# Input norm from row sums of 32 columns and a first conditioning chunk loaded ahead of the activations, in a one-core transformer layer

## The chip, the core and the metric

The kernel runs on one core of a Trainium2 chip. The metric is the device time of one execution in microseconds, from the start of the program to its end. All data is f32, and an f32 matmul appears in the trace as two passes (two MATMUL records with two weight loads).

## What is computed

One layer of a diffusion backbone over 256 latent tokens and 256 context tokens of width 1024: a modulated RMS norm, three token mixing branches (neighbourhood attention, a gated scan, grouped-query attention) from one projection, a gated merge, and then a mixture of 16 experts with the top 2 per token. The change touches only the very first step:

```python
mod   = split((silu(c)     @ w_ada + b_ada), 6)      # c: conditioning of the sample
mod_c = split((silu(c_ctx) @ w_ada + b_ada), 6)      # c_ctx: that of the context
h_lat = modulate(rmsnorm(x,   g_mix), mod[0],   mod[1])
h_ctx = modulate(rmsnorm(ctx, g_mix), mod_c[0], mod_c[1])
# rmsnorm(x, g) = x * rsqrt(mean(x*x) + 1e-6) * g ;  modulate(h, shift, scale) = h * (1 + scale) + shift
y_lat = token_mixer(h_lat, h_ctx, w_in, ...)
```

## The kernel before, in words

Everything is written out by hand: five instruction streams (SyncE issues the large transfers, GpSimd, ScalarE, TensorE, VectorE), held together by semaphores. Each stream runs strictly in its written order, so a wait holds back all that is written behind it on that engine.

The activations of both token sets lie transposed in `hT`: 128 partitions, 8 slices k of the width, 512 tokens (256 latent, 256 context). The front works like this:

- Transfers (L418 to L425, SyncE): four chunks of `xcT` (two slices k each, 512 KB), and then, four times, a conditioning chunk `ada_mix[g]` (2048 KB, the weights that give shift and scale for the slices 2g and 2g+1) with a quarter of the first projection's weights, "ff" (512 KB). The conditioning vectors `cvec` and the first part of the small tables come over ScalarE's queue (L598, L599).
- Squares: ScalarE squares the even slices (L602), VectorE the odd ones (L1285), into `sq`.
- Sums: TensorE sums over the 128 partitions by a matmul with a 128 x 128 block of ones (L998), 8 slices into `pv_bank`. Every partition of the result holds the sum of all 512 tokens.
- Root and reciprocal: ScalarE takes `sqrt(sum/1024 + eps)` over 512 columns (L609), VectorE the reciprocal of 512 columns (L1287). Before, ScalarE has turned `cvec` into its Silu (L604) and has loaded the table of Sqrt with an operation on one column (L606).
- Conditioning: `mix(g)` (L977) is 8 matmuls with 32 columns of weights, in four column groups of the array side by side, over 512 moving columns; ScalarE copies the result out of the bank (L614), `mix_turn(g)` (L986) turns it by four transposes, and VectorE makes from it the shift `mod` and the factor `A_mix` (L1310 to L1316).
- Norm and modulation (VectorE): each slice times the reciprocal row (L1308), then times factor plus shift for the two halves of the tokens (L1321), which raises `h_ready`.
- The first projection, "ff" (L1019): for each k four matmuls i of 512 columns; `mix(g+1)` is put behind the first of them in a group of two slices, `mix_turn(g+1)` ahead of the next k. The matmul i = 3 of k = 0 writes `pv_bank` and waits until ScalarE has read it (`rms_root`).
- Matmuls without use (`warm_up`, L993: ones times zeros, 256 columns) fill TensorE's pauses; WARM gives their numbers, 7 ahead of the sums, 4 behind them, 1 behind `mix(0)`, 3 behind its turn.

Behind the ff projection TensorE goes on without a break into the next projections (L793, L797, L801), the scan and the attention, the merge (L814, L820), the gather (L1140) and the experts (L1180). In the attention, L965 multiplies with 64 columns of weights over 128 moving columns, two halves of the array side by side.

Of the kernel before, what the change touches and what calls it, by code (L numbers as in the profile page):

```python
# [13 lines left out]
P = 128  # L14
# [72 lines left out]
WARM = (7, 4, 1, 3)  # L87
# [55 lines left out]
def build(nc, d):  # L143

    ctx = ExitStack()
    with ctx:
# [46 lines left out]
        rstd_row = at(C0, 512)  # L193
        QR = at(C0 + 1024, 4, L)
# [96 lines left out]
        def sem(name):  # L291
            return ctx.enter_context(nc.semaphore(name))
# [10 lines left out]
        pass_in = [[sem(f"pass_in{m}{e}") for e in range(2)] for m in range(3)]  # L303
# [7 lines left out]
        ones_set = sem("ones_set")  # L311
        lb_in, lb_ready = sem("lb_in"), sem("lb_ready")
# [77 lines left out]
        def _(sp):  # L390
# [26 lines left out]

            for i in range(4):  # L418
                sp.dma_start(hT[:, 2 * i:2 * i + 2, :], d["xcT"][:, 2 * i:2 * i + 2, :]).then_inc(x_in[i], 16)
            for g in range(MIXES):  # L420
                sp.dma_start(ada_mix[g].rearrange("p a b -> p (a b)"), d["ada_mix"][g, :, :]).then_inc(mix_in[g], 16)
                cols = slice(1024 * g, 1024 * g + 1024)
                sp.dma_start(slot[0][:, cols], d["front_w"][0, :, cols]).then_inc(ff_in[g], 16)
                if g == 1:
                    sp.dma_start(small[:, SMALL_FIRST:SMALL], d["small_w"][:, SMALL_FIRST:SMALL]).then_inc(small_in, 16)  # L425
# [72 lines left out]
            with sp.If(n_pass > 1):  # L498
                with sp.Fori(1, n_pass) as p:
                    with sp.Fori(0, PAIRS) as j:  # L500
                        sp.wait_ge(down_ready, (p * PAIRS + j) * 2)
                        for m in range(3):
                            for e in range(2):
                                sp.dma_start(slot[PASS_SLOTS[m][e]], d["expert_w"][bass.ds(j * 6 + (3 * e + m), 1), :, :]
                                             .rearrange("a p n -> p (a n)")).then_inc(pass_in[m][e], 16)
# [91 lines left out]
        def _(act):  # L597
            act.dma_start(cvec, d["cvec"]).then_inc(c_in, 16)  # L598
            act.dma_start(small[:, 0:SMALL_FIRST], d["small_w"][:, 0:SMALL_FIRST]).then_inc(first_in, 16)  # L599
            for k in range(0, KD, 2):  # L600
                act.wait_ge(x_in[k // 2], 16)
                act.activation(sq[:, k, :], hT[:, k, :], ACT.Square).then_inc(sq_by["act"], 1)  # L602
# [3 lines left out]
            act.activation(warm, ones_now[:, 0:1], ACT.Sqrt)  # L606
            act.wait_ge(rms_ready, 1)
            act.wait_ge(first_in, 16)
            act.activation(rstd_row, pv_bank[:, :], ACT.Sqrt, bias=sm("eps"), scale=1.0 / D).then_inc(rms_root, 1)  # L609
            for g in range(MIXES):  # L610
                act.wait_ge(mix_ready, g + 1)
                if g > 1:
                    act.wait_ge(shared_ready, shared_no("mix", g - 2) + 1)
                act.activation(ada_rows[:, g % 2, :], score[g % 2][:, :], ACT.Copy).then_inc(mix_out, 1)  # L614

# [156 lines left out]
        def _(pe):  # L772
# [221 lines left out]

            warm_up(WARM[0])
            for k in range(KD):
                pe.wait_ge(sq_by["dve" if k % 2 else "act"], k // 2 + 1)
                ins = pe.matmul(pv_bank[:, :], ones_now, sq[:, k, :], start=(k == 0), stop=(k == KD - 1))  # L998
            ins.then_inc(rms_ready, 1)
            warm_up(WARM[1])  # L1000
            pe.wait_ge(c_ready, 1)
            pe.wait_ge(first_in, 16)
            mix(0)
            warm_up(WARM[2])
            mix_turn(0)
            warm_up(WARM[3])
            for k in range(KD):
# [4 lines left out]
                for i in range(4):  # L1012
                    if (k % MIX_K, i) == (0, 1) and g + 1 < MIXES:
                        mix(g + 1)
                    if (k % MIX_K, i) == (1, 0) and g + 1 < MIXES:
                        mix_turn(g + 1)
                    if k == 0 and i == 3:
                        pe.wait_ge(rms_root, 1)
                    ins = pe.matmul(banks[BANK_OF[i]][:, :], lhs(slot[0], k, i * P), hT[:, k, :],  # L1019
                                    start=(k == 0), stop=(k == KD - 1))  # L1020
                    if k == KD - 1:
                        ins.then_inc(fill_ready, 1)
# [144 lines left out]
            def retake(m, n):  # L1167

                for e in range(2):
                    pe.wait_ge(pass_in[m][e], n * 16 - 16 * LAST)  # L1170
# [97 lines left out]
        def _(dve):  # L1268
# [14 lines left out]
            for k in range(1, KD, 2):  # L1283
                dve.wait_ge(x_in[k // 2], 16)
                dve.tensor_tensor(sq[:, k, :], hT[:, k, :], hT[:, k, :], ALU.mult).then_inc(sq_by["dve"], 1)  # L1285
            dve.wait_ge(rms_root, 1)
            link(dve.reciprocal(rstd_row, rstd_row))  # L1287
# [17 lines left out]
            for g in range(MIXES):  # L1305
                ks = slice(MIX_K * g, MIX_K * g + MIX_K)
                for k in range(KD)[ks]:
                    dve.tensor_tensor(hT[:, k, :], hT[:, k, :], rstd_row, ALU.mult)  # L1308
# [10 lines left out]
                for k in range(KD)[ks]:  # L1319
                    for s in range(2):  # L1320
                        ins = dve.tensor_scalar(hT[:, k, s * L:(s + 1) * L], hT[:, k, s * L:(s + 1) * L],  # L1321
                                                A_mix[:, k, s:s + 1], mod[:, k, s:s + 1], ALU.mult, ALU.add)
                    ins.then_inc(h_ready, 1)
# [649 lines left out]
```

## Time and profile before

| | us |
|---|---|
| median of 3 runs | 721.85 (721.7 to 723.26) |
| the profiled execution, its time | 723.5 |
| its span, first to last instruction | 721.6 |
| TensorE busy | 696.8 |
| first ff matmul starts | 20.3 |

In the rows below, a line such as L1019 is the line of the program that issued the instruction; `xN` counts instructions (passes, for f32 matmuls). "PE" is TensorE's matmuls and "PEld" its weight loads, DVE is VectorE, ACT ScalarE, POOL GpSimd, SP SyncE; a "q" behind an engine is its sequencer. Times are microseconds from the start of the span, unless marked ns. [...] Ends of matmuls are modelled, and consecutive matmuls overlap in the records.

### The profile page before, as it was taken

How to read it: one execution, taken by the hardware profiler on the slowest of the kernel's cores; microseconds unless marked ns; L12 is line 12 of the kernel's file. 1: busy time of each engine (PE TensorE's matmuls, PEld its weight loads, DVE VectorE, ACT ScalarE, POOL GpSimd, SP SyncE). 2: the span in 40 equal slices, each digit the busy share in tenths (PEclk: the TensorE clock that was granted, in tenths of full speed). 3: DMA queues.
4: the chain of work that ended last, by engine and by line, in shares of the span. 5: the costliest groups of instructions: out<-in, count | busy, mean ns of one | idle time of the engine just before them, and what ended most of it. 6: DMA issues, size and time to landing. Idle time of an engine off the chain costs nothing.

```text
span 721.6 us, 8021 instructions
## 1 busy us (share of the span) xinstructions
PE 696.8 (97%) x3274; PEld 416.5 (58%) x3274; DVE 288.9 (40%) x505; ACT 114.5 (16%) x199; POOL 179.5 (25%) x128
## 2 busy tenths in 40 slices
PE   9999999999999999998999999998999999999994
PEld 5444586555775457777777878647444434434431
DVE  3339392677210475743343233325323113202315
ACT  4021011111000422221121240013000000000004
POOL 0008998799079000800000000000000000000013
PEclk9999999999999999999999999998999999999997
DMA  9994526762432332433471235997799999999992
GB/s 357 418 379 181 211 108 234 291 219 71 175 134 100 116 118 69 165 116 117 175 288 54 79 121 191 421 404 310 283 417 423 419 423 421 420 421 421 420 408 85
DMA packets 29509, 183.70 MB, mean 255 GB/s; under 512 B 3543, under 2 KB 5975, under 8 KB 14624
## 3 DMA queue, kind: packets, MB, share of 16 engines
q1 hardware_dynamic: 27600, 178.98, 62.5%
q0 software_dynamic: 1584, 3.97, 1.4%
q8 instruction: 27, 0.44, 0.2%
q10 hardware_dynamic: 288, 0.23, 0.1%
q14 instruction: 10, 0.08, 0.0%
HBM read 178.14 MB, written 6.82 MB: 256 GB/s over the span
## 4 chain that ended last, share of the span: by engine, by line
PE 90%; DMA 3%; DVE 2%; issue 1%; POOL 1%; ACT 1%; DVEq 0%; SPq 0%; POOLq 0%; ACTq 0%
PE bank L1180 20%; PE bank L797 18%; PE bank L801 10%; PE bank L793 8%; PE bank L814 6%; PE bank L1140 4%; PE bank L1019 4%; PE bank L820 4%; PE bank L944 2%; PE bank L965 2%; PE bank L846 2%; PE bank L952 2%; PE bank L807 2%; DMA y_rows<-sb,token_rows 1%; DMA sb<-y_rows 1%
## 5 line engine op out<-in xcount | busy, mean ns | idle before, releaser
L1180 PE MATMUL bank<-sb 128*64 128x512 f32 x768 | 166.8, 594 | 0.7 <-ACT sb L728 0.7
L797 PE MATMUL bank<-sb 128*128 128x256 f32 x576 | 128.5, 382 | 0.6 <-PE bank L793 0.3
L797 PEld LDWEIGHTS bank<-sb 128*128 128x128 f32 x576 | 108.3, 190 | 17.6 <-issue 3.8
L1180 PEld LDWEIGHTS bank<-sb 128*64 128x64 f32 x768 | 53.9, 137 | 106.9 <-issue 105.0
L583 POOL DMA_INDIRECT y_rows<-sb,token_rows x7 | 7.0, 1000 | 373.0 <-DVE sb L1737 373.0
L543 POOL TENSOR_TENSOR sb<-sb 128x1024 f32<-128x1024 f32 x32 | 67.4, 2108 | 58.7 <-DMA sb<-ada_w 36.4
L1369 DVE COPY sb<-bank 128x512 f32<-128x512 f32 x45 | 29.2, 685 | 104.6 <-PE bank L952 66.1
L801 PE MATMUL bank<-sb 128*128 128x512 f32 x160 | 70.2, 594 | 0.3 <-PE bank L797 0.3
L793 PE MATMUL bank<-sb 128*128 128x512 f32 x128 | 55.8, 593 | 0.3 <-PE bank L1019 0.3
L801 PEld LDWEIGHTS bank<-sb 128*128 128x128 f32 x160 | 29.9, 191 | 35.2 <-issue 35.2
L1702 DVE TENSOR_TENSOR sb<-sb,bank 128x512 f32<-128x512 f32 x8 | 5.5, 687 | 97.1 <-PE bank L1180 97.1
L814 PE MATMUL bank<-sb 128*128 128x256 f32 x192 | 42.2, 381 | 0.6 <-PE bank L814 0.6
L793 PEld LDWEIGHTS bank<-sb 128*128 128x128 f32 x128 | 24.0, 190 | 29.3 <-issue 29.3
L814 PEld LDWEIGHTS bank<-sb 128*128 128x128 f32 x192 | 36.3, 190 | 6.3 <-issue 1.5
L547 POOL TENSOR_TENSOR sb<-sb 128x512 f32<-128x512 f32 x24 | 36.0, 1501 | 1.9
L1140 PE MATMUL bank<-sb 128*128 128x128 f32 x256 | 34.5, 294 | 0.0
L1140 PEld LDWEIGHTS bank<-sb 128*128 128x128 f32 x256 | 32.6, 208 | 0.1
L548 POOL TENSOR_TENSOR sb<-sb 128x512 f32<-128x512 f32 x24 | 31.8, 1323 | 1.9
L1693 DVE TENSOR_SCALAR sb<-bank,sb 128x128 f32<-128x128 f32 x64 | 21.9, 403 | 21.8 <-PE bank L1140 21.8
L1019 PE MATMUL bank<-sb 128*128 128x512 f32 x64 | 29.0, 599 | 0.7 <-DVE sb L1321 0.7
L683 ACT ACTIVATE sb<-bank,sb 128x512 f32<-128x512 f32 x32 | 21.8, 685 | 40.9 <-DVE sb L1484 40.8
L820 PE MATMUL bank<-sb 128*128 128x512 f32 x64 | 27.8, 592 | 0.0
(246 smaller groups left out, 674.3 us busy)
## 6 DMA issues: line engine op xcount, KB each, us to landing
sb<-expert_w SPq DMA_DIRECT2D x90, 1024.0 KB, 19.4
sb<-front_w SPq DMA_DIRECT2D x19, 2048.0 KB, 8.2
sb<-ada_w SPq DMA_DIRECT2D x32, 512.0 KB, 3.3
sb<-ada_mix SPq DMA_DIRECT2D x4, 2048.0 KB, 19.6
sb<-expert_w SPq DMA_DIRECT2D x12, 512.0 KB, 11.0
sb<-xcT SPq DMA_DIRECT2D x4, 512.0 KB, 6.3
sb<-front_w SPq DMA_DIRECT2D x4, 512.0 KB, 20.3
y_rows<-sb SPq DMA_DIRECT2D x4, 512.0 KB, 23.8
```

The lines of the kernel that those rows point to most:

```text
L543: link(pool.tensor_tensor(w, w, cvec[:, k0:k0 + PART_K, 0:1].broadcast_to([P, PART_K, 512]), ALU.mult))
L547: link(pool.tensor_tensor(w[:, 0, :], w[:, 0, :], w[:, 1, :], ALU.add))
L548: ins = pool.tensor_tensor(ada_sum[g], ada_sum[g], w[:, 0, :], ALU.add)
L793: ins = pe.matmul(ps[:, :], lhs(w, k, i * P), hT[:, k, :], start=(k == 0), stop=(k == KD - 1))
L797: ins = pe.matmul(ps[:, c * L:(c + 1) * L], lhs(w, k, (2 * i + c) * P), hT[:, k, 0:L], start=(k == 0), stop=(k == KD - 1))
L801: ins = pe.matmul(ps[:, :], hT[:, k, i * P:(i + 1) * P], w[:, k * 512:(k + 1) * 512], start=(k == 0), stop=(k == KD - 1))
L814: ins = pe.matmul(ps[:, c * L:(c + 1) * L], lhs(w, k, (2 * i + c) * P, D), src[:, k, :], start=(k == 0), stop=(k == 3))
L820: ins = pe.matmul(ps[:, :], yT[:, k, i * P:(i + 1) * P], w[:, k * 512:(k + 1) * 512], start=(k == 0), stop=(k == KD - 1))
L1019: ins = pe.matmul(banks[BANK_OF[i]][:, :], lhs(slot[0], k, i * P), hT[:, k, :], start=(k == 0), stop=(k == KD - 1))
L1140: ins = pe.matmul(banks[i][:, c * P:(c + 1) * P], x_nat[:, t, (4 * i + c) * P:(4 * i + c + 1) * P], S[:, t, :], start=(t == 0), stop=(t == ...
L1180: ins = pe.matmul(bank[e * CAP:(e + 1) * CAP, :], lhsT[:, k, e * CAP:(e + 1) * CAP], weights_at(k, e), start=(k == 0), stop=(k == parts - 1))
L1369: dve.tensor_copy(dst, shared_wait(n)[:, :]).then_inc(shared_out, 1)
```

## The change

1. `ada_mix[0]` is issued ahead of the four `xcT` chunks; the other chunks stay where they were.
2. On ScalarE, Silu of `cvec` and the copy of the first mix come ahead of the squares. The Sqrt table is loaded behind the last square.
3. On TensorE, `mix(0)` and its turn come ahead of the sums. The sums use 32 columns of ones: four matmuls for each k, one for each tile of 128 tokens, each into its own 32 partitions of `pv_bank`, columns 0 to 127. Partition 32b + j holds the sums of token tile b.
4. Root and reciprocal are taken of these 128 columns (`rstd_parts`). Four matmuls, whose weights are one column of the identity repeated 128 times, spread each tile's row over all partitions, back into `pv_bank` as 512 columns.
5. VectorE makes the vectors of the first group ahead of its last two squares; it multiplies the first two slices straight from `pv_bank`, one slice at a time with its modulation behind a drain. The others use `rstd_row`, to which ScalarE copies the bank once the two slices are done.
6. In the ff loop `mix(1)` stands at k = 1, i = 0 and its turn at k = 1, i = 2, in place of k = 0, i = 1 and k = 1, i = 0. The matmul i = 3 of k = 0 now waits for the copy to `rstd_row`.
7. WARM becomes (10, 1, 1, 4, 4): 10 ahead of `mix(0)`, 1 behind it, 1 ahead of each even k of the sums, 4 behind the sums, 4 behind the spread.
8. In the loop for further passes of the experts, the two semaphores of each weight pair are merged to one.

```diff
 FILLS = [f for g in FRONT if g[:3] != "out" for f in group_fills(g)]
 FILLS += [(f"out{i}", t, "dve") for t in range(NT) for i in range(2)]
 PBANKS = 3
-WARM = (7, 4, 1, 3)
+WARM = (10, 1, 1, 4, 4)
 BANK_OF = [7 if f[:2] == ("ff", 3) else n % PBANKS for n, f in enumerate(FILLS)]
 ROW_GROUPS = (4, 5, 10, 11)
 POOLED = (6, 7, 8, 9, 4, 5, 10, 11)
...
         b_rows = at(F0, 2, 512)
         C0 = F0 + 8192
         rstd_row = at(C0, 512)
+        rstd_parts = at(F0 + 2 * SLOT - P, P)
         QR = at(C0 + 1024, 4, L)
         row5 = at(C0 + 1024, D)
         v_hg = at(C0 + 2048, 4, 512)
...
                 for e in range(2):
                     load_unit(2 * q + e)
 
+            sp.dma_start(ada_mix[0].rearrange("p a b -> p (a b)"), d["ada_mix"][0, :, :]).then_inc(mix_in[0], 16)
             for i in range(4):
                 sp.dma_start(hT[:, 2 * i:2 * i + 2, :], d["xcT"][:, 2 * i:2 * i + 2, :]).then_inc(x_in[i], 16)
             for g in range(MIXES):
-                sp.dma_start(ada_mix[g].rearrange("p a b -> p (a b)"), d["ada_mix"][g, :, :]).then_inc(mix_in[g], 16)
+                if g:
+                    sp.dma_start(ada_mix[g].rearrange("p a b -> p (a b)"), d["ada_mix"][g, :, :]).then_inc(mix_in[g], 16)
                 cols = slice(1024 * g, 1024 * g + 1024)
                 sp.dma_start(slot[0][:, cols], d["front_w"][0, :, cols]).then_inc(ff_in[g], 16)
                 if g == 1:
...
         def _(act):
             act.dma_start(cvec, d["cvec"]).then_inc(c_in, 16)
             act.dma_start(small[:, 0:SMALL_FIRST], d["small_w"][:, 0:SMALL_FIRST]).then_inc(first_in, 16)
-            for k in range(0, KD, 2):
-                act.wait_ge(x_in[k // 2], 16)
-                act.activation(sq[:, k, :], hT[:, k, :], ACT.Square).then_inc(sq_by["act"], 1)
             act.wait_ge(c_in, 16)
             act.activation(cvec, cvec, ACT.Silu).then_inc(c_ready, 1)
             act.wait_ge(ones_set, 1)
-            act.activation(warm, ones_now[:, 0:1], ACT.Sqrt)
-            act.wait_ge(rms_ready, 1)
-            act.wait_ge(first_in, 16)
-            act.activation(rstd_row, pv_bank[:, :], ACT.Sqrt, bias=sm("eps"), scale=1.0 / D).then_inc(rms_root, 1)
-            for g in range(MIXES):
+
+            def mix_copy(g):
+
                 act.wait_ge(mix_ready, g + 1)
                 if g > 1:
                     act.wait_ge(shared_ready, shared_no("mix", g - 2) + 1)
                 act.activation(ada_rows[:, g % 2, :], score[g % 2][:, :], ACT.Copy).then_inc(mix_out, 1)
+
+            mix_copy(0)
+            for k in range(0, KD, 2):
+                act.wait_ge(x_in[k // 2], 16)
+                act.activation(sq[:, k, :], hT[:, k, :], ACT.Square).then_inc(sq_by["act"], 1)
+            act.activation(warm, ones_now[:, 0:1], ACT.Sqrt)
+            act.wait_ge(rms_ready, 1)
+            act.wait_ge(first_in, 16)
+            act.activation(rstd_parts, pv_bank[:, 0:P], ACT.Sqrt, bias=sm("eps"), scale=1.0 / D).then_inc(rms_root, 1)
+            act.wait_ge(rms_spread, 1)
+            act.wait_ge(h_ready, MIX_K)
+            act.activation(rstd_row, pv_bank[:, :], ACT.Copy).then_inc(rstd_ready, 1)
+            for g in range(1, MIXES):
+                mix_copy(g)
 
             act.wait_ge(lb_in, 1)
             act.activation(lb_e, lb_e, ACT.Exp).then_inc(lb_ready, 1)
...
                     pe.matmul(banks[2][:, 0:256], ones_now, zeros, start=True, stop=True)
 
             warm_up(WARM[0])
+            pe.wait_ge(c_ready, 1)
+            mix(0)
+            warm_up(WARM[1])
+            pe.wait_ge(first_in, 16)
+            mix_turn(0)
             for k in range(KD):
+                if k % 2 == 0:
+                    warm_up(WARM[2])
                 pe.wait_ge(sq_by["dve" if k % 2 else "act"], k // 2 + 1)
-                ins = pe.matmul(pv_bank[:, :], ones_now, sq[:, k, :], start=(k == 0), stop=(k == KD - 1))
+                for b in range(4):
+                    ins = pe.matmul(pv_bank[32 * b:32 * b + 32, 0:P], ones_now[:, 0:32], sq[:, k, P * b:P * b + P],
+                                    start=(k == 0), stop=(k == KD - 1))
             ins.then_inc(rms_ready, 1)
-            warm_up(WARM[1])
-            pe.wait_ge(c_ready, 1)
-            pe.wait_ge(first_in, 16)
-            mix(0)
-            warm_up(WARM[2])
-            mix_turn(0)
             warm_up(WARM[3])
+            pe.wait_ge(rms_rec, 1)
+            for b in range(4):
+                ins = pe.matmul(pv_bank[:, P * b:P * b + P], ident[:, 32 * b:32 * b + 1].broadcast_to([P, P]), rstd_parts,
+                                start=(b == 0), stop=(b == 3))
+            ins.then_inc(rms_spread, 1)
+            warm_up(WARM[4])
             for k in range(KD):
                 g = k // MIX_K
                 pe.wait_ge(h_ready, k + 1)
                 if k % 2 == 0:
                     pe.wait_ge(ff_in[k // 2], 16)
                 for i in range(4):
-                    if (k % MIX_K, i) == (0, 1) and g + 1 < MIXES:
+                    if (k % MIX_K, i) == ((0, 1) if g else (1, 0)) and g + 1 < MIXES:
                         mix(g + 1)
-                    if (k % MIX_K, i) == (1, 0) and g + 1 < MIXES:
+                    if (k % MIX_K, i) == ((1, 0) if g else (1, 2)) and g + 1 < MIXES:
                         mix_turn(g + 1)
                     if k == 0 and i == 3:
-                        pe.wait_ge(rms_root, 1)
+                        pe.wait_ge(rstd_ready, 1)
                     ins = pe.matmul(banks[BANK_OF[i]][:, :], lhs(slot[0], k, i * P), hT[:, k, :],
                                     start=(k == 0), stop=(k == KD - 1))
                     if k == KD - 1:
...
 
             def retake(m, n):
 
-                for e in range(2):
-                    pe.wait_ge(pass_in[m][e], n * 16 - 16 * LAST)
+                pe.wait_ge(pass_in[m], n * 32 - 32 * LAST)
 
             def two_experts(bank, weights_at, parts, lhsT, q=None, n=None):
 
...
 
             dve.memset(zeros, 0.0)
             dve.memset(ones_now, 1.0).then_inc(ones_set, 1)
-            for k in range(1, KD, 2):
+            def square(k):
+
                 dve.wait_ge(x_in[k // 2], 16)
                 dve.tensor_tensor(sq[:, k, :], hT[:, k, :], hT[:, k, :], ALU.mult).then_inc(sq_by["dve"], 1)
-            dve.wait_ge(rms_root, 1)
-            link(dve.reciprocal(rstd_row, rstd_row))
 
             def add_ada(g):
 
...
 
             b_ada = sm("b_ada")
             dve.wait_ge(first_in, 16)
-            for g in range(MIXES):
+
+            def mix_vectors(g):
+
                 ks = slice(MIX_K * g, MIX_K * g + MIX_K)
-                for k in range(KD)[ks]:
-                    dve.tensor_tensor(hT[:, k, :], hT[:, k, :], rstd_row, ALU.mult)
                 parts = shared_wait(shared_no("mix", g))[:, :].rearrange("p (c q s) -> p c s q", c=4, q=4)[:, :, 0:2, :]
                 dve.tensor_reduce(mod[:, ks, :], parts[:, 0:2], AX.X, ALU.add)
                 link(dve.tensor_reduce(mod[:, KD + MIX_K * g:KD + MIX_K * g + MIX_K, :], parts[:, 2:4], AX.X, ALU.add))
...
                 link(dve.scalar_tensor_tensor(out=A_mix[:, ks, :], in0=mod[:, KD + MIX_K * g:KD + MIX_K * g + MIX_K, :], scalar=1.0,
                                               in1=sm("g_mix")[:, ks].unsqueeze(2).broadcast_to([P, MIX_K, 2]),
                                               op0=ALU.add, op1=ALU.mult))
-                for k in range(KD)[ks]:
-                    for s in range(2):
-                        ins = dve.tensor_scalar(hT[:, k, s * L:(s + 1) * L], hT[:, k, s * L:(s + 1) * L],
-                                                A_mix[:, k, s:s + 1], mod[:, k, s:s + 1], ALU.mult, ALU.add)
-                    ins.then_inc(h_ready, 1)
+
+            def normed_row(k, row):
+                dve.tensor_tensor(hT[:, k, :], hT[:, k, :], row, ALU.mult)
+
+            def normed_rows(g, row):
+
+                for k in range(MIX_K * g, MIX_K * g + MIX_K):
+                    normed_row(k, row)
+
+            def modulated_row(k):
+
+                for s in range(2):
+                    ins = dve.tensor_scalar(hT[:, k, s * L:(s + 1) * L], hT[:, k, s * L:(s + 1) * L],
+                                            A_mix[:, k, s:s + 1], mod[:, k, s:s + 1], ALU.mult, ALU.add)
+                ins.then_inc(h_ready, 1)
+
+            def modulated(g):
+
+                for k in range(MIX_K * g, MIX_K * g + MIX_K):
+                    modulated_row(k)
+
+            square(1)
+            square(3)
+            mix_vectors(0)
+            square(5)
+            square(7)
+            dve.wait_ge(rms_root, 1)
+            dve.reciprocal(rstd_parts, rstd_parts).then_inc(rms_rec, 1)
+            dve.wait_ge(rms_spread, 1)
+            for k in range(MIX_K):
+                normed_row(k, pv_bank[:, :])
+                dve.drain()
+                modulated_row(k)
+            dve.wait_ge(rstd_ready, 1)
+            for g in range(1, MIXES):
+                normed_rows(g, rstd_row)
+                mix_vectors(g)
+                modulated(g)
             dve.wait_ge(small_in, 16)
             lg = sm("lb")
             dve.tensor_tensor(lb_e, lg, lg, ALU.subtract).then_inc(lb_in, 1)
```

## Rows read from the trace of the kernel before

**Rows 1.** The page: busy time by engine, then the last-ended chain by engine.
```profile
PE 696.8 (97%) x3274; PEld 416.5 (58%) x3274; DVE 288.9 (40%) x505; ACT 114.5 (16%) x199; POOL 179.5 (25%) x128
...
PE 90%; DMA 3%; DVE 2%; issue 1%; POOL 1%; ACT 1%; DVEq 0%; SPq 0%; POOLq 0%; ACTq 0%
```

**Rows 2.** The chain in order of time, 8 to 60 us: start, length, what.
```profile
12.02 1.28 ACT L606
...
13.52 0.58 ACT sb L609
...
14.13 3.36 DVE sb L1287
...
17.51 1.29 DVE sb L1308 x2
...
19.52 0.75 DVE sb L1321 x2
...
20.31 1.12 PE bank L1019 x2
21.44 1.85 PE bank L977 x16
...
26.06 0.44 PE bank L986 x4
26.50 4.29 PE bank L1019 x10
...
30.79 1.85 PE bank L977 x16
```

**Rows 3.** Two lines of transfers: fourth x chunk, then all conditioning chunks; start, us to landing.
```profile
L419 SPq DMA_DIRECT2D sb<-xcT x1: 790/790/790, 2.1 to 2.1; - x1
...
DMA to landing us min/median/max: 7.5/7.5/7.5
...
L421 SPq DMA_DIRECT2D sb<-ada_mix x4: 432/524/654, 3.0 to 6.8; - x4
...
DMA to landing us min/median/max: 11.5/19.6/29.4
```

**Rows 4.** Timeline of TensorE, first 20 us: start, length, line, tile, form, count.
```profile
1.34 4.70 PE L993 MATMUL bank<-sb 128*128 128x256 f32 x14 [1.34 <-DVE sb L1282]
...
14.98 1.92 PE L977 MATMUL bank<-sb 128*32 128x512 f32 x16
...
17.62 0.66 PE L986 MATMUL bank<-sb 128*128 128x128 f32 x4
```

**Rows 5.** Groups by line and form, 0 to 60 us: busy, mean ns, idle before.
```profile
L1287 DVE RECIPROCAL sb<-sb 128x512 f32<-128x512 f32 x1 | 3.4, 3353 | 3.8 <-ACT sb L609 3.8
...
L602 ACT ACTIVATE sb<-sb 128x512 f32<-128x512 f32 x4 | 2.5, 630 | 4.8 <-DMA sb<-xcT 4.8
L614 ACT ACTIVATE sb<-bank 128x512 f32<-128x512 f32 x4 | 2.4, 597 | 26.2 <-PE bank L977 26.2
...
L609 ACT ACTIVATE sb<-bank,sb 128x512 f32<-128x512 f32 x1 | 0.7, 669 | 0.0
...
L1328 DVE RECIPROCAL sb<-sb 128x8 f32<-128x8 f32 x1 | 0.2, 204 | 0.3 <-ACT sb L617 0.3
```

**Rows 6.** Timeline of TensorE near 415 us, in the attention.
```profile
415.99 1.09 PE L965 MATMUL bank<-sb 128*64 128x128 f32 x16 [1.01 <-DVE sb L1369]
```

**Rows 7.** The chain of the whole span, a later gather.
```profile
523.44 1.79 PE bank L1140 x16
```

**Rows 8.** Timeline of VectorE at 711 to 716 us; a drain lies between.
```profile
711.95 2.48 DVE L1719 TENSOR_TENSOR sb<-sb,bank 128x512 f32<-128x512 f32 x4 [2.23 <-POOL sb L592]
714.52 1.29 DVE L1712 TENSOR_TENSOR sb<-sb 128x512 f32<-128x512 f32 x2
```

**Rows 9.** TensorE's timeline at 489 to 515 us, then one stretch's busy times and clock.
```profile
498.64 0.41 PE L1124 MATMUL bank<-sb 128*128 128x32 f32 x2 [1.85 <-DVE sb L1624]
...
500.05 6.65 PE L1140 MATMUL bank<-sb 128*128 128x128 f32 x32
...
499.00:500.00 1.00, 1.00 (x7) 0.96 (x6) 0.67 (x3) 0.15 (x1) 0.00 (x0) 0.58 0.88 250
```

## What the change does to the time: the prediction

> **What bounds the kernel now.** I read the page first. TensorE (PE) is busy 97% of the span and holds 90% of the chain that ended last; VectorE (DVE) is busy 40% and ScalarE (ACT) 16% [rows 1]. So only what moves TensorE's stream of matmuls counts. The change sits in the first 30 us, and there I read the chain [rows 2]: Sqrt table load (1.28 us), root over 512 columns (0.58), reciprocal (3.36), two row products (1.29), modulation vectors (18.80 to 19.52), first modulated row (0.75). The first "ff" matmul (L1019) starts at 20.31, and from there TensorE hardly pauses before 685 us. So the number to predict is how much earlier or later that matmul starts, plus any new hole in the first two groups behind it. What follows is released by TensorE, the expert loads too. What is tied to the early transfers has slack: the last conditioning chunk lands at 6.8 + 29.4 = 36.2 [rows 3]; its products come at 26.50 + 4.29 + 9.35 = 40.1, where 9.35 is the period of a group (21.44 to 30.79) [rows 2].
>
> **Transfers.** The last x chunk lands at 2.1 + 7.5 = 9.6, conditioning chunk 0 behind it at 3.0 + 11.5 = 14.5 [rows 3], in queue order. The x chunks are 4 x 512 KB, a conditioning chunk is 2048 KB, so the swap exchanges the times: chunk 0 at 9.6, the last x chunk at 14.5, the x chunks before it about 1.25 apart, everything later unchanged. SP issues the same transfers, and only their order is new. The norm is released 4.9 us later; in return the mix products, their turn and the vectors leave the path behind it.
>
> **Conditioning in front.** `mix(0)` starts at 9.65 and takes 1.92 [rows 4], to 11.6. The copy on ACT takes 0.60 [rows 5], to 12.25. The turn starts at 12.3 and issues in 0.44 [rows 2], to 12.75. The vectors on DVE (about 0.8 with their reduces) are done by 13.8, ahead of the last x chunk, which hides them. Queued behind ACT's new wait for `mix_ready` are its squares: those for k = 0, 2, 4 run 12.25 to 14.15 (3 x 0.63, [rows 5]), done before 14.5. So this wait costs nothing; had the mix come 0.4 us later, it would start to.
>
> **Row sums.** For each k there are now four matmuls with 32 columns of weights and 128 tokens: 8 passes (an f32 matmul is two). No row shows this shape. The nearest is L965, the same 128 moving columns on half the array: 16 passes in 1.09, so 0.064 each with two side by side, 0.13 a round [rows 6]. With four side by side it is two rounds, 0.26 per k. Low bound 0.21 (two passes at a quarter of the 0.43 of a 512 column pass, 4.29 for ten); high bound 8 x 0.064 = 0.51. I take 0.26, since L977 does run four 32 column groups side by side: 16 passes of 512 columns in 1.85 [rows 2], not in 16 x 0.43. On PE follow behind the turn: four warm-ups of 0.43 and eight k of 0.26, 12.75 + 1.7 + 2.1 = 16.5; with 0.2 for the end of the pipeline `rms_ready` comes at 16.7. The last squares are there at 14.5 + 0.69 = 15.2, so PE and not the data sets this.
>
> **Root.** The Sqrt table load used to lie beside the old sums. Now it stands behind the last square: 14.5 + 0.63 + 1.28 + 0.1 = 16.55, just under the sums' 16.7. The root over 512 columns takes 0.67 [rows 5] and an ACT operation on one column 0.20 (L606, 13.31 to 13.52, ahead of the root in [rows 2]); 128 columns make 0.32, I take 0.35, to 17.05. The row-wide copy to `rstd_row` is new but beside the path: it waits for two modulated rows, ends near 22.9, and PE wants it at its fourth matmul, at 20.95 + 3 x 0.86 = 23.5. If it came later, PE would wait for the difference.
>
> **Reciprocal.** 3.353 us for 512 columns and 0.204 for 8 [rows 5] make 6.25 ns a column, 0.95 for 128: done at 18.05. That is the real saving, 2.4 us. But PE has four warm-ups queued behind the sums, 16.5 + 1.7 = 18.2: 0.15 of them is on the path.
>
> **Spreading by products.** Four f32 products are 8 passes of 128 columns. L986 does 4 passes, from first issue to last end, in 0.66 [rows 4]; four more at 0.112 (16 in 1.79, [rows 7]) make 1.1, with bounds of 0.9 and 1.3. Done at 19.3.
>
> **First row.** Product 0.69 (1.29 for two, overlapping, [rows 2]), drain 0.09 (L1719 ends at 714.43, L1712 behind a drain starts at 714.52, [rows 8]), two modulations 0.75: 19.35 + 1.53 = 20.9. The last four warm-ups end at 18.2 + 0.9 + 1.7 = 20.8 and just fit. The ff matmuls start at 20.95 in place of 20.31: **+0.65 us**.
>
> **Order of chunk 1.** `mix(1)` moves behind the four matmuls of k = 0. It had no wait to lose: 20.31 + 1.12 = 21.43, and it runs at 21.44 [rows 2]. Its turn is now covered by two matmuls (1.71 us) instead of four. DVE needs about 1.55 from the end of a turn to `h_ready` (reduces 0.1, vectors 0.7, modulation 0.75), and the turn lasts 0.2 beyond its issue: a hole of 0.05. The merged pass semaphores stand in the loop for further passes, which the expert loads (96 MB, each weight once) show not to run: nothing.
>
> Sum: 0.65 + 0.05 = +0.7. The profiled execution has a span of 721.6 and a time of 723.5, 1.65 above the median; on its span this makes 722.3, on the median of 721.85 it makes 722.5.
>
> [...] The Sqrt table load runs 12.02 to 13.30, and of the time to the root at 13.52 the 0.20 of L606 leaves 0.02 [rows 2]. [...]
>
> **Rivals.**
> A (15%, slower). [...]
> [...]
> B (10%, slower). The small sums don't pack: 0.51 per k, sums done at 18.5, +2.0 on the forecast, 724.5. From 0.25 per k on PE is behind ACT, and every 0.1 costs 0.8. For: the shape is in no row. Against: L977.
> C (8%, faster). Data and fixed costs come in better. 2 MB of x and some small tables take 9.6 us, the next 2 MB only 4.9 [rows 3], so 4 us are start-up; if the larger rows of the conditioning chunk shorten it by 1 us, all shifts by 1: 721.5. With sums and spread at their low ends (-0.25 -0.2) and no late warm-up on the path (-0.15, and two queues fewer to hand over), 720.5.
> D (2%, slower). The swap doesn't do what it says: the transfers share the queues, chunk 0 lands near 14 anyway, and mix, copy, squares and sums follow it. +4 to +5, 726.
>
> **How the numbers follow.** Forecast 65%: 722.5, own range 721 to 723.3 (sum bounds and the 0.2% by which runs differ). The range 720.8 to 725.5 takes in B, the milder part of C and the low edge of A. A measurement can tell about 0.2% (1.4 us) from no change. Faster by more: C but 1%, 0.07. Slower by more: A, B and D but 3% of mild ends, 0.24. Same: 0.69.
>
> **What the profile will show.** Right: L977's first group near 9.7, the last square ending near 15.1 with the table load behind it, a reciprocal of 0.95 at 17 to 18, the first ff matmul at 20.9, full clock up to 50 us. Wrong: a granted clock of 0.5 in the front or ff passes twice as long (A), sums past 17.5 (B), a last x chunk before 14 or a start before 19.8 (C), a mix after 12 (D), a hole of over 0.3 ahead of k = 2.

## The result and the profile after

Over 20 runs each, the changed kernel takes 724.15 us in the median (722.85 to 725.86) and the kernel before 722.56 us (721.35 to 724.45). The ratio is 1.0018, 95% interval 1.0009 to 1.0026: slower by 1.6 us by the medians (0.22%) and by 1.3 us by the ratio, at the edge of the 0.2% (1.4 us) named as the bound. The range of the prediction, 720.8 to 725.5, holds the time. The likeliest value, 722.5, lay 1.65 us too low; 0.7 of that is the base, since the three runs shown beforehand had put the median of before at 721.85, and 0.9 is the change itself (+0.7 against +1.6).

The page of the changed kernel, busy time and then the chain that ended last by engine, answers to [rows 1]:

```profile
PE 698.3 (97%) x3346; PEld 418.0 (58%) x3346; DVE 291.0 (40%) x505; ACT 113.4 (16%) x199; POOL 179.0 (25%) x128
```

TensorE has 72 passes more (the new products and fillers) and still sets everything. Where the time went stands in the chain of the front (start, length, what; L1006 are the warm-ups, L990 mix, L999 turn, L1019 row sums, L1025 spread, L1041 ff), which answers to [rows 2]:

```profile
0.75 8.08 DMA sb<-cvec
...
8.85 0.42 ACT sb L605
...
9.32 1.97 PE bank L990 x16
...
12.12 0.63 PE bank L999 x4
12.75 0.43 PE bank L1006 x2
13.18 0.57 PE bank L1019 x16
13.76 0.63 PE bank L1006 x2
14.38 0.57 PE bank L1019 x16
...
16.79 0.57 PE bank L1019 x16
17.36 1.92 PE bank L1006 x8
19.29 0.89 PE bank L1025 x8
20.18 1.73 PE bank L1006 x8
21.91 3.57 PE bank L1041 x8
25.48 1.85 PE bank L990 x16
...
29.68 2.76 PE bank L1041 x6
32.44 1.86 PE bank L990 x16
```

From 12.12 on the chain never leaves TensorE: turn, fillers, sums, fillers, spread, fillers. The last activation chunk, the table load and the reciprocal don't appear in it at all. Only at its end does this view say too much: ends of matmuls are modelled, and the weight load of the first ff matmul, which starts ahead of the 21.91 of the chain, waited for VectorE's modulated row and not for the fillers (the timeline of TensorE's weight loads):

```profile
21.78 0.30 PEld L1041 LDWEIGHTS bank<-sb 128*128 128x128 f32 x2 [0.27 <-DVE sb L1351]
```

The first ff matmul starts at 21.78 (its first weight load; 20.31 before), `mix(2)` at 32.44 (30.79 before): +1.47 and +1.65. I laid the two chains beside each other as far as the router, and this difference of 1.65 stays in every stage to 393 us (the second projection starts at 57.47 against 55.82); near 395 us TensorE waits once more for VectorE (0.30), and the difference is 2.0 from there to the router at 498 us. So up to there nothing gives the front's delay back. In the two profiled executions the spans differ by only 0.4 us (722.0 against 721.6), since the difference drops to 0.4 in the router, where the clock falls at another moment; more on this at the end.

The timeline of ScalarE in the changed kernel, with the last square, the table load and the root:

```profile
14.55 0.63 ACT L618 ACTIVATE sb<-sb 128x512 f32<-128x512 f32 x1 [0.65 <-DMA sb<-xcT]
15.20 1.28 ACT L619 ACT_TABLE_LOAD   x1
16.49 0.20 ACT L619 ACTIVATE sb<-sb 128x1 f32<-128x1 f32 x1
17.43 0.37 ACT L622 ACTIVATE sb<-bank,sb 128x128 f32<-128x128 f32 x1 [0.74 <-PE bank L1019]
```

The last chunk is there at 14.5, as worked out, but the root waits 0.74 us for the sums. The table is ready at 16.5 and the sums are not before 17.4.

### The profile page after: what moved, and what is told of

The parts are those of the page before. It is cut to its first block, busy times and chain, and to the rows that moved or that the text cites. A ratio compares the mean times of both kernels' runs of the same rounds, so it can differ in the third digit from the quotient of the medians.

```text
span 722.0 us, 8171 instructions
## 1 busy us (share of the span) xinstructions
PE 698.3 (97%) x3346; PEld 418.0 (58%) x3346; DVE 291.0 (40%) x505; ACT 113.4 (16%) x199; POOL 179.0 (25%) x128
## 4 chain that ended last, share of the span: by engine, by line
PE 92%; DMA 4%; issue 1%; DVE 1%; POOL 1%; ACT 0%; DVEq 0%; POOLq 0%; ACTq 0%
PE bank L1201 20%; PE bank L810 18%; PE bank L814 10%; PE bank L806 8%; PE bank L827 6%; PE bank L1162 4%; PE bank L1041 4%; PE bank L833 4%; PE bank L978 2%; PE bank L957 2%; PE bank L859 2%; PE bank L965 2%; PE bank L820 2%; DMA sb<-y_rows 2%; DMA sb<-cvec 1%
## 5 line engine op out<-in xcount | busy, mean ns | idle before, releaser
L810 PEld LDWEIGHTS bank<-sb 128*128 128x128 f32 x576 | 108.1, 190 | 17.8 <-issue 3.8
L814 PEld LDWEIGHTS bank<-sb 128*128 128x128 f32 x160 | 29.8, 190 | 35.3 <-issue 35.3
L806 PEld LDWEIGHTS bank<-sb 128*128 128x128 f32 x128 | 23.9, 190 | 29.3 <-issue 29.3
L827 PEld LDWEIGHTS bank<-sb 128*128 128x128 f32 x192 | 36.2, 190 | 6.3 <-issue 1.5
L1162 PE MATMUL bank<-sb 128*128 128x128 f32 x256 | 31.7, 278 | 0.3 <-issue 0.3
L1162 PEld LDWEIGHTS bank<-sb 128*128 128x128 f32 x256 | 29.8, 192 | 0.4 <-issue 0.4
L1746 DVE TENSOR_SCALAR sb<-bank,sb 128x128 f32<-128x128 f32 x64 | 21.9, 405 | 19.0 <-PE bank L1162 19.0
L1041 PE MATMUL bank<-sb 128*128 128x512 f32 x64 | 29.2, 600 | 0.0
```

The lines of the kernel that those rows point to most:

```text
L806: ins = pe.matmul(ps[:, :], lhs(w, k, i * P), hT[:, k, :], start=(k == 0), stop=(k == KD - 1))
L810: ins = pe.matmul(ps[:, c * L:(c + 1) * L], lhs(w, k, (2 * i + c) * P), hT[:, k, 0:L], start=(k == 0), stop=(k == KD - 1))
L814: ins = pe.matmul(ps[:, :], hT[:, k, i * P:(i + 1) * P], w[:, k * 512:(k + 1) * 512], start=(k == 0), stop=(k == KD - 1))
L827: ins = pe.matmul(ps[:, c * L:(c + 1) * L], lhs(w, k, (2 * i + c) * P, D), src[:, k, :], start=(k == 0), stop=(k == 3))
L1162: ins = pe.matmul(banks[i][:, c * P:(c + 1) * P], x_nat[:, t, (4 * i + c) * P:(4 * i + c + 1) * P], S[:, t, :], start=(t == 0), stop=(t == ...
```

## The experiments

Two questions were open. Which of three things sets the new start: TensorE's own queue of fillers (theory Q), the table load behind the last square (L), or the swap with its late last chunk (S)? And what does each half of the change do alone (rival P: both gain by themselves)? "ff" below is the start of the first ff matmul, "mix(2)" that of the third conditioning product, where the hole ahead of k = 2 (a wait of TensorE for VectorE) is in. Both are of the profiled execution. Each ratio is taken against runs of the kernel before from the same session, whose median was 722.0 in the experiments (722.5 for the last row), so the medians of the table can't be divided by 722.56. The medians of the experiments rest on 8 to 12 runs each, that of the swap alone on two.

| kernel | ff | mix(2) | median, us | ratio to before |
|---|---|---|---|---|
| before | 20.31 | 30.79 | 722.56 | |
| changed | 21.78 | 32.44 | 724.15 | 1.0018 (1.0009 to 1.0026) |
| no fillers between the sums | 20.74 | 31.40 | 722.26 | 1.0002 (0.9992 to 1.0011) |
| Sqrt table early | 22.0 | 32.67 | 723.63 | 1.0023 (1.0010 to 1.0036) |
| both, fewer fillers | 19.83 | 30.49 | 721.10 | 0.9985 (0.9975 to 0.9995) |
| norm part alone | 20.86 | 31.34 | 722.46 | 1.0001 (0.9992 to 1.0010) |
| swap alone | 25.84 | 36.51 | 728.23 | 1.0084 (1.0063 to 1.0106) |
| no fillers behind the mix | 19.88 | 31.96 | 723.89 | 1.0028 (1.0017 to 1.0039) |
| norm alone, Sqrt before Silu | 19.70 | 30.37 | 720.33 | 0.9989 (0.9977 to 1.0000) |
| the same, mix chunk in halves | 19.18 | 29.84 | 720.21 | 0.9974 (0.9964 to 0.9984) |
| the same, other order, six fillers in the router | 19.28 | 29.76 | 721.46 | 0.9992 (0.9982 to 1.0002) |
| the same, other order, router as it was | 19.11 | 29.59 | 720.87 | 0.9976 (0.9964 to 0.9988) |

**No fillers between the sums.**

```diff
-WARM = (10, 1, 1, 4, 4)
+WARM = (10, 1, 0, 4, 4)
```

> The changed kernel without the four warm-ups between the row sums (WARM[2] = 0). In the changed kernel the ff matmuls start at 21.78 us, the row sums end at 17.36. Theory Q (TensorE's own queue of filler matmuls sets the end of the sums): the last squares are there at 15.24, the sums end near 15.9, the root then waits for the Sqrt table (16.7), reciprocal done at 18.05, the four warm-ups behind the sums end by 17.8 and are off the path, the spread ends at 19.0, ff starts at 20.5 to 20.7, 1.1 to 1.3 us earlier than in the changed kernel: about 723.0 against 722.6 of before. 
Its chain, behind the landing of the last chunk at 14.5 (L622 root, L1366 reciprocal):

```profile
15.18 1.28 ACT L619
...
16.68 0.27 ACT sb L622
...
16.97 0.96 DVE sb L1366
...
17.98 1.16 PE bank L1025 x8
19.14 1.73 PE bank L1006 x8
20.86 3.57 PE bank L1041 x8
```

Q holds. The start moves 1.04 us ahead, a little less than the 1.1 expected at least: the reciprocal is done at 17.93, 0.12 ahead of what I had, but the spread takes 1.16 behind a TensorE that had been idle, in place of the 0.89 behind the fillers of the changed kernel. (The weight load of ff waited 0.27 us for VectorE here too, so the four fillers behind the spread cost nothing.) The table load, absent from the chain of the changed kernel, is now in it. The granted clock, as a share of full speed, doesn't fall (1.00 in every stretch to 26 us). The median can't be told from that of before.

**Sqrt table early.**

```diff
+            act.activation(warm, ones_now[:, 0:1], ACT.Sqrt)
             mix_copy(0)
             for k in range(0, KD, 2):
...
-            act.activation(warm, ones_now[:, 0:1], ACT.Sqrt)
             act.wait_ge(rms_ready, 1)
```

> The changed kernel with the one-column Sqrt (and so its table load) ahead of the first mix copy instead of behind the last square. Theory Q: the table was loaded at 16.5 and the sums ended at 17.4, so nothing moves, ff start 21.8 within 0.1 us, time as the changed kernel (724.15, ratio to before 1.002). Theory L (ScalarE's order with the table load behind the last square sets the root): ff starts 0.7 us earlier. A copy or a square that needs a table of its own would show as a further table load.

ScalarE's timeline:

```profile
9.57 1.28 ACT L615 ACT_TABLE_LOAD   x1
...
14.62 0.63 ACT L619 ACTIVATE sb<-sb 128x512 f32<-128x512 f32 x1 [0.65 <-DMA sb<-xcT]
17.65 0.37 ACT L622 ACTIVATE sb<-bank,sb 128x128 f32<-128x128 f32 x1 [2.40 <-PE bank L1019]
```

L falls for the changed kernel: ScalarE is free 2.4 us ahead of the root and gains nothing. The start is 0.2 later, as `cvec` landed 0.3 later here (9.12 against 8.83). Copy and Square needed no table of their own behind Sqrt: the next table load stands at 44.56 (L630).

**Both edits, and WARM = (10, 1, 0, 2, 3).**

> Both edits, and only two warm-ups behind the sums and three behind the spread. Theory Q with L as the next limit: sums end near 15.9, root at 15.9 to 16.3, reciprocal to 17.25, spread to 18.2, first row to 19.75: ff starts at 19.8, 0.5 us earlier than before the change and 2.0 earlier than in the changed kernel. The hole ahead of k = 2 (0.18) stays. Time 722.2, ratio to before 0.9995, to be told from the changed kernel's 1.0018. Theory S: no earlier than 21. Theory A: half clock in the front and a start later than 21.

```profile
14.50 0.43 PE bank L1019 x8
...
14.95 0.69 PE bank L1019 x16
...
15.66 0.38 ACT sb L622
...
16.06 0.96 DVE sb L1366
...
17.07 1.17 PE bank L1025 x8
...
18.26 0.69 DVE sb L1341
...
19.83 3.70 PE bank L1041 x8
```

The start is as expected to 0.03 us, with some luck in it. The sums that start at 14.50 are those of k = 5; the last chunk had landed at 14.25, 0.3 sooner than in the changed kernel:

```profile
14.27 0.63 ACT L619 ACTIVATE sb<-sb 128x512 f32<-128x512 f32 x1 [0.56 <-DMA sb<-xcT]
```

So from the last chunk to ff this chain takes 5.6 us, and with a landing at 14.5 the start would be near 20.1, as an estimate from these rows, 0.2 us ahead of before. S, which saw no start before 21, falls. The time follows, and by more than expected (0.9985 for 0.9995): it lies apart from the changed kernel's 1.0018.

**The norm part alone**, on the kernel before: sums, root and reciprocal as changed, the spread ahead of `mix(0)`, a copy to `rstd_row`, transfers and Silu untouched.

```diff
+            pe.wait_ge(rms_rec, 1)
+            for b in range(4):
+                ins = pe.matmul(pv_bank[:, P * b:P * b + P], ident[:, 32 * b:32 * b + 1].broadcast_to([P, P]), rstd_parts,
+                                start=(b == 0), stop=(b == 3))
+            ins.then_inc(rms_spread, 1)
             pe.wait_ge(c_ready, 1)
             mix(0)
```

> The norm part alone on the kernel before: transfers, Silu and first mix stay where they were, the sums take 32 columns, root and reciprocal 128, four products spread them (ahead of the first mix on TensorE), ScalarE copies the row. If each part acts by itself (rival P: the norm part is the gain, the swap is the loss), ff starts 1.5 us or more before 20.3 and the time is 721 or less. By my reading the mix chunk lands at 14.5 and mix, copy, turn, vectors and one modulation behind it take 4.9 us, so the start can't come before 19.4; with the spread ahead of the mix on TensorE until 15.7 it is 20.4, no change: 722.6, ratio 1.000.

```profile
14.87 1.13 PE bank L1010 x8
16.00 1.90 PE bank L981 x16
...
20.86 1.13 PE bank L1031 x2
```

P falls. The reciprocal costs 2.4 us less and the start is 0.55 later than before (0.45 later than I had it): the spread (L1010) stands in TensorE's queue until 16.0 ahead of a mix that had started at 14.98 [rows 4], and the conditioning chain behind it sets the start. The median doesn't tell this kernel from before.

**The swap alone**: the changed kernel with 128 columns of ones in the sums, root and reciprocal over 512 columns, WARM = (10, 1, 0, 12, 0).

> The swap alone: conditioning chunk 0 ahead of the x chunks, first mix, its turn and vectors ahead of the norm, but sums with 128 columns of ones, root and reciprocal over 512 columns as before the change (twelve warm-ups behind the sums, none between). By the rows: turn issued by 12.75, eight sums of 0.86 end at 19.6, root 0.67 to 20.3, reciprocal 3.36 to 23.7, product and modulation 1.5: ff starts at 25.2, 4.9 us later than before. Rival P (both parts gain by themselves): a start before 20.3.

```profile
13.06 6.95 PE bank L1015 x16
...
20.75 3.36 DVE sb L1356
...
25.84 3.70 PE bank L1031 x8
```

5.5 us later than before (4.9 expected; the turn ended 0.3 later; the drain, 0.08 between product and modulation, and the hand-overs make most of the rest). The time of 1.0084 rests on two runs, 726.8 and 729.7, so I go by the starts. The parts aren't additive: the swap costs 5.5 us with the old norm and 0.9 with the new one (20.86 to 21.78), and the new norm is worth 4.1 us behind the swap and costs 0.55 without it.

**No fillers behind the first mix**: Sqrt early, WARM = (10, 0, 0, 0, 0).

> The changed kernel with the Sqrt table early and no warm-up behind the first mix at all (10, 0, 0, 0, 0). The chain itself then ends as in the kernel with both edits: ff starts at 19.8. Theory A (the fillers hold the clock): TensorE is thinly used from 11.5 to 19.8, its clock falls to a half there, the first ff passes take 0.43 instead of 0.21 us, and the group ahead of k = 2 ends 2 to 3.5 us later than 30.2; time 723 to 725. If the clock stays, 721.0, as with both edits.

Stretches of the front (busy PE, PEld, DVE, ACT, POOL with counts, then the granted clock, DMA share, GB/s), and its chain:

```profile
16.00:18.00 2.00, 0.88 (x8) 0.89 (x8) 0.95 (x1) 0.08 (x1) 0.00 (x0) 1.00 1.09 467
18.00:20.00 2.00, 0.40 (x4) 0.21 (x2) 1.60 (x4) 0.00 (x0) 0.00 (x0) 0.84 0.89 363
20.00:22.00 2.00, 2.00 (x3) 0.97 (x4) 1.20 (x4) 0.60 (x1) 0.00 (x0) 0.50 1.02 414
22.00:24.00 2.00, 2.00 (x5) 0.77 (x5) 1.25 (x2) 0.00 (x0) 0.00 (x0) 0.81 1.14 479
...
19.88 5.12 PE bank L1041 x8
```

The half clock that the prediction names as A's sign, shown: TensorE does 0.88 and 0.40 us of work in two stretches of 2 us, then the granted clock falls from 1.00 to 0.50, and the first eight ff passes take 5.12 us instead of the 3.70 of the kernel with both edits, a loss of 1.4 us (I expected 2 to 3.5). The ratio is 1.0028 with the same chain ahead of ff that gave 0.9985 with fillers. Of these 2.8 us between the medians `mix(2)` shows 1.5; another 0.4 appears between 124 and 186 us and the rest isn't explained. So the fillers in the front earn their place, but not those between the sums: their removal alone brought no fall.

**Norm alone, Sqrt ahead of Silu.** From the norm part alone: the root and its table before Silu, so the spread is done before the mix chunk lands; `mix(1)` ordered as in the change; WARM = (7, 2, 1, 3, 1), which is two fillers fewer behind the sums and one more behind the spread.

> The norm part alone, as before, but with root ahead of Silu on ScalarE (its table is loaded while the sums run), the spread done by 14.1 ahead of the mix, and mix(1) behind k = 0. The mix chunk lands at 14.5 and sets the rest: mix to 16.5, copy to 17.2, turn to 17.9, vectors to 18.6, modulation to 19.4: ff starts at 19.45, 0.85 before 20.31; with the hole of 0.18 ahead of k = 2 0.7 us are left: 721.4 to 721.6 on a median of 722.0 to 722.3 for before. If the spread or the fillers stand in the mix's way, 20.0.

The start is 19.70: the spread took 1.13 and the filler behind it 0.43, so the mix began at 14.83. The time goes with it, 0.9989, though its interval touches 1.

**The mix chunk in two halves**, with a semaphore each, no filler ahead of the mix:

```diff
+                    for h, done in enumerate((mix_half, mix_in[0])):
+                        sp.dma_start(ada_mix[0][:, 4 * h:4 * h + 4, :].rearrange("p a b -> p (a b)"),
+                                     d["ada_mix"][0, :, 2048 * h:2048 * h + 2048]).then_inc(done, 16)
```

> The same with conditioning chunk 0 in two transfers of 1024 KB with a semaphore each, and no warm-up ahead of the mix. The first half lands near 12.1, so its four matmuls (0.93 us) run from 14.05, and only the second half's 0.93 us stands behind the landing at 14.5: the mix ends at 15.9, ff starts at 18.8, 1.5 us earlier than before, 1.3 with the hole: 720.7 to 721.0. If the landing of the second half is late, or the chain behind is bound by another engine, no earlier than 19.4.

```profile
13.19 1.13 PE bank L1018 x8
14.32 1.90 PE bank L989 x16
...
19.18 3.70 PE bank L1039 x8
```

Start 19.18, 0.4 later than I had it (the spread again ran to 14.32), and 1.1 us ahead of before. The ratio is 0.9974: faster than before and than the change.

**The other order of mix(1), and six fillers in the router.**

```diff
-                    if (k % MIX_K, i) == ((0, 1) if g else (1, 0)) and g + 1 < MIXES:
+                    if (k % MIX_K, i) == ((0, 1) if g else (0, 3)) and g + 1 < MIXES:
...
-            keep_warm(2)
+            keep_warm(6)
```

> The split-mix kernel with mix(1) ahead of k = 0, i = 3 and its turn at k = 1, i = 1 (three ff matmuls cover the vectors in place of two), and six useless matmuls in place of two in front of the position sums near 497 us. The hole of 0.18 ahead of k = 2 goes. Theory R (the runs of one kernel differ by 1.3 to 3 us because TensorE's clock falls in the router at a moment that changes from run to run, and TensorE idles 1.85 us there): with the idle time filled the falls get rarer or shorter, the runs lie closer together, median 719.6 to 719.8. If the fillers delay the position sums: 1.5 us later. If R is wrong, the spread stays 1.5 to 3 us.

The hole is gone: 19.28 to 29.76 is 10.48 us, against 10.66 in the kernel with the mix chunk in halves. The fillers in the router stand in the chain (L1096), and the clock had fallen ahead of them, as the stretch below the chain's lines shows (busy times, then the granted clock, here 0.74):

```profile
497.08 3.75 PE bank L1096 x12
500.84 0.14 PE bank L1144 x2
...
492.00:493.00 1.00, 1.00 (x9) 1.00 (x8) 0.00 (x0) 0.98 (x2) 0.00 (x0) 0.74 1.00 418
```

They ran mostly at half clock (12 passes in 3.75 us, 0.31 each; 0.22 at full clock, 8 in 1.73 in the changed kernel's front) and held back the position sums (L1144). The fall came between 492 and 493 us, with TensorE busy and about 4 us before the first of them, so they could not prevent it.

**The changed kernel with six fillers in the router.**

> The changed kernel with six useless matmuls in place of two in front of the position sums near 499 us, nothing else. Its 20 runs lay at 722.9 to 723.1, 723.9 to 724.3 and 725.4 to 725.9. Theory R (a fall of the clock in the router at a moment that changes from run to run makes these steps): the upper steps get rare, the median falls from 724.15 to 723.0, and against before the ratio is then about 1.001 or less. If R is wrong, the steps and the median stay.

Median 724.28, ratio 1.0029 (1.0020 to 1.0038), runs again near 722.9, 724.2 and 725.8. The steps and the median stay, which is what I had named as the sign against R. It refutes the remedy, but it doesn't test R: here too the clock fell between 495 and 496 us, ahead of the fillers at 500.5.

**The other order without these fillers.**

> The split-mix kernel with mix(1) ahead of k = 0, i = 3 and its turn at k = 1, i = 1, without the fillers of the run before. ff starts at 19.2; in the run before the group from there to mix(2) took 10.48 us against 10.66 in the split-mix kernel, so mix(2) should start at 29.7, 1.1 us earlier than before the change, and the median should lie 1.1 to 1.7 us below before: ratio 0.998, range 0.9965 to 0.9990. If what helped was chance in the runs of the split-mix kernel, 1.000.

0.9976 (0.9964 to 0.9988), `mix(2)` at 29.59, 1.2 us ahead of before. It can't be told from the split kernel by its time; the hole that the other order closes is 0.18 us.

## Why the prediction was right, and where its terms were off

- **The number.** 724.15 lies in the wide range but outside the forecast's own range of 721 to 723.3. What held it was the room left for rivals A and B, and neither happened: the granted clock is 1.00 in every stretch of the changed kernel's front, and the small sums pack. That part is luck. What follows is the sum's own account: it had ff at 20.95, and it came at 21.78.
- **What bounds it, and that the delay carries through.** Right. 1.65 us at 32 us are 1.65 us at 375, and 1.6 in the median. The 0.35 near 395 us was not foreseen, and why VectorE is late there stays open.
- **Rival A.** The ten warm-ups ended at 8.50 and the mix began at 9.32, so TensorE was idle for 0.8 us, less than I had reckoned with. In the kernel without fillers it was idle there for 1.55 us, and the granted clock stayed at 1.00 until 18 us. The 15% for A, and its low edge at which the range ends (725.5), were my estimates; no run shows a fall at that price. Where the clock did fall in the front, without the fillers, it cost 1.4 us in the first ff passes, and the median was 723.89.
- **Transfers.** The last x chunk landed at 14.5 as worked out. Chunk 0 came at 0.75 + 7.9 = 8.65, 1 us sooner than the 9.6 assumed, but the small `cvec` fell behind it: 8.83 instead of 0.7 + 4.9 = 5.6, and Silu and the mix waited for that. The two misses cancel: the turn was issued by 12.75, the number predicted. I hadn't asked what the swap does to the transfers of ScalarE's queue. Why `cvec` waited longer there no run separates; none varied the packet size alone.
- **Row sums.** 0.57 for two k, 0.285 each against 0.26: right, rival B is refuted, though the sums ended near its sign of 17.5. The term that failed is the four fillers among them, taken as 0.43 each. They cost 0.63 wherever a group of sums with 32 columns comes before them. The chain says it: the first filler, behind the turn, still takes 0.43, the next three 0.63, the four behind the sums 1.92 instead of 1.72. Ahead of the end of the sums that is 0.6 us in three places, and with the sums' 0.2 it brings 17.36 in place of 16.5: nearly the whole of the 0.83 us by which ff came late against the sum. Why a filler comes late there no run separates.
- **Root and reciprocal.** 0.37 and 0.95, as said. The table load was not the limit, but by 0.7 us and not by a hair.
- **Fillers behind the sums.** They end at 19.28, 0.5 us behind the reciprocal (18.78), but the spread behind them is shorter by most of that. It ends 1.40 us behind the reciprocal here and 1.21 in the kernel without fillers between the sums, where nothing stood in its way. Their price is 0.2, near the 0.15 predicted.
- **Spread and first row.** 0.89 instead of 1.1, as the weight loads ran ahead behind the fillers: they begin at 18.91, the last filler ends at 19.28 (1.16 in the kernel without fillers between the sums, where TensorE had been idle and loads and matmuls both start at 17.98); the row 1.5 as said. The last fillers do "just fit": the chain has them end at 21.9, but the weight load of ff had waited 0.27 us for VectorE, and from the end of the spread to ff it takes 1.60 us with four of them and 1.59 with three.
- **Order of chunk 1.** A hole as predicted, 0.18 instead of 0.05.
- **Table load.** The load takes 1.28 us and no more: in the changed kernel it starts 0.02 behind the last square (15.20), and the one-column Sqrt 0.01 behind its end (16.49). The Silu and Sqrt loads of the other runs, too, are followed within 0.02 us where the operand was there (12.15 + 1.28 to 13.45 with Sqrt ahead of Silu).

In one sentence: the mechanism (TensorE's own queue of sums and fillers, and not the data, sets the root, and eats the saving) was right, and its size was too small by 0.2 us for each of three changes from 32 column sums to a full width filler and by 0.2 for the sums.

## What to carry to other kernels

A filler matmul is an instruction in a queue. Count it at the price that it has behind its neighbours, and look in the chain whether fillers appear there, then whether the next wanted instruction really waited for them. Three groups stand in the chain here: dropping the one between the sums brought 1.0 us, the one behind the sums cost 0.2, and the last cost nothing. Without the first, with the others trimmed and one table load moved ahead, ff started 2.0 us sooner. Before swapping two transfers, work out the chain behind each when it is the last to land. Here it takes 5.6 us behind the activations and 4.9 from the start of a mix in the unsplit kernel, and the starts are near each other (19.83 and 19.70), so the order decides little; what pays is to have the other chain quite done before the last landing, and to cut the last transfer so that part of its work runs ahead. And where fillers are cut, one step too many takes back what the others gave (1.0028 after 0.9985): look at the granted clock.

## What the runs showed of the hardware

- An f32 matmul is two records with two weight loads: the 8 matmuls of `mix(0)` are 16 passes in the chain, and the page counts 3346 of PE and 3346 of PEld.
- A full width matmul behind a group of 32 column matmuls comes 0.2 us late (0.63 for 0.43, three times; 1.92 for 1.72, in the changed kernel). The same is in the kernel before: 2.77 for six ff passes behind a mix (10 take 4.29, so six take 2.57).
- Four matmuls of 32 columns over 128 tokens run side by side: 8 passes in 0.285 us, 0.036 each, against 0.112 for a full width pass of 128 columns (16 in 1.79, [rows 7]).
- With a 2048 KB transfer issued first, in place of one of 512 KB, a 128 KB one issued on another queue at the same time lands later: after 8.1 to 8.4 us in the kernels with the swap, after 4.8 to 5.0 in those without.
- The runs of one kernel lie in steps (the changed one: near 722.9, 724.2, 725.7). They seem to go with the clock in the router, where it falls in 11 of the 13 profiled executions. I took the time of each less its shift at `mix(2)`, leaving out the two kernels with six fillers. Where the half clock there didn't come or was over in under 4 us, this is 720.8 to 722.0 (five kernels); where it lasted almost 7 us, 722.0 to 724.0 (six kernels, the kernel before among them, whose gather ran at half clock [rows 9]). The two groups touch at 722.0. That the fall makes the steps is argued from these eleven executions and not shown; the fillers meant to remove it came behind the fall, and what would keep the clock up there stays open.
